# A hybrid diffusion backbone on one core: the heads of the differential form first, and the latent form's preparation beside them through one PSUM bank

## What is computed

```python
def mla_mixer(...):                     # latent form
    q = (rms_norm(c_q, g_q) @ w_uq).reshape(B, L, 4, 64 + 32)
    kv = (rms_norm(c_kv, g_kv) @ w_ukv).reshape(B, L, 4, 64 + 64)
    q_nope, q_rope = q[..., :64], q[..., 64:]
    k_nope, v = kv[..., :64], kv[..., 64:]
    # rope_2d on q_rope and k_rope for latent tokens; k_rope is shared by the heads
    # softmax(q k^T * 96 ** -0.5) v, per head
def diff_mixer(...):                    # differential form
    lam = exp(sum(lq1 * lk1)) - exp(sum(lq2 * lk2)) + lambda_init
    # 8 sub-heads of 32: rope_2d on q and k for latent tokens, softmax for each
    o = o[:, :, 0] - lam * o[:, :, 1]   # two sub-heads make one head
```

## Time and profile before

| what | value |
|---|---|
| median of 3 runs | 3166.14 us (3163.36 to 3167.25) |
| the profiled execution's own time | 3168.7 us |
| its span | 3166.9 us |
| PE, DVE, ACT, POOL busy | 80%, 62%, 37%, 36% of the span |
| attention block, layer 0 | 367.6 to 537.1 us |
| attention block, layer 1 | 2288.7 to 2395.0 us |

### The profile page before, as it was taken

How to read it: one execution, slowest core, us unless ns; L and a number is a source line. 1 busy time by engine, 2 the same in 40 slices (tenths; PEclk the granted TensorE clock), 3 DMA queues, 4 the chain that set the end, 5 groups by cost and what they waited for, 6 DMA issues and landing times. The chain is left out here.

```text
span 3166.9 us, 41622 instructions
## 1 busy us (share of the span) xinstructions
PE 2542.6 (80%) x15562; PEld 1901.4 (60%) x15562; DVE 1975.4 (62%) x4467; ACT 1168.2 (37%) x2244; POOL 1133.9 (36%) x1013
## 2 busy tenths in 40 slices
PE   5978699899166777888789999888777797777776
PEld 3778546587166777777678777577745552222222
DVE  3566535478896899877744444466543799845544
ACT  3422235327682333333333333342234443333332
POOL 1024100331006676566565555202303354433331
PEclk8985689899598898998899999888678899999999
DMA  5210141147039999999999999631002799999996
GB/s 206 77 31 1 62 160 36 60 150 251 0 166 381 407 406 403 365 384 397 390 400 406 405 406 405 242 97 31 9 1 90 302 415 422 421 422 422 421 421 247
DMA packets 211896, 816.93 MB, mean 258 GB/s; under 512 B 22680, under 2 KB 41688, under 8 KB 178032
## 3 DMA queue, kind: packets, MB, share of 16 engines
q0 software_dynamic: 110592, 536.92, 41.9%
q1 hardware_dynamic: 101104, 277.35, 23.5%
HBM read 796.37 MB, written 17.83 MB: 257 GB/s over the span
## 5 line engine op out<-in xcount | busy, mean ns | idle before, releaser
L1978 PE MATMUL ps<-pair_ring,pair_diag 128*128 128x512 f32 x1024 | 476.3, 610 | 144.4 <-ACT pair_diag L2052 141.7
L2162 DVE CUSTOM_DVE_ANT_0 pair_ring<-pair_ring,hT 128x1024 f32<-128x1024 f32 x256 | 313.1, 1223 | 212.0 <-DMA pair_ring<-in_uv_rows,eid 203.7
L1978 PEld LDWEIGHTS ps<-pair_ring,pair_diag 128*128 128x128 f32 x1024 | 187.2, 192 | 423.4 <-ACT pair_diag L2052 227.5
L1942 POOL DMA_INDIRECT pair_ring<-in_uv_rows,eid x256 | 267.4, 1045 | 391.7 <-PE ps L1978 366.8
L2310 POOL DMA_INDIRECT sparse_ring<-in_v_rows,eidT x256 | 286.0, 1117 | 294.9 <-PE ps L2359 223.0
L2310 POOL DMA_INDIRECT sparse_ring<-in_u_rows,eid x256 | 349.2, 1364 | 113.9 <-issue 67.5
L119 PE MATMUL ps<-h_hi,peer_uh 128*128 128x256 f32 x1024 | 310.6, 303 | 83.7 <-DVE peer_ul L2422 76.0
L2448 DVE CUSTOM_DVE_ANT_0 sparse_ring<-sparse_ring,hT 128x1024 f32<-128x1024 f32 x256 | 303.8, 1222 | 40.4 <-DMA sparse_ring<-in_u_rows,eid 32.9
L120 PE MATMUL ps<-h_lo,peer_uh 128*128 128x256 f32 x1024 | 300.0, 293 | 1.1 <-issue 1.1
L121 PE MATMUL ps<-h_hi,peer_ul 128*128 128x256 f32 x1024 | 299.3, 292 | 0.0
L119 PEld LDWEIGHTS ps<-h_hi,peer_uh 128*128 128x128 f32 x1024 | 206.8, 202 | 147.3 <-DVE peer_ul L2422 94.9
(11 more groups left out here) (413 smaller groups left out, 5437.6 us busy)
## 6 DMA issues: line engine op xcount, KB each, us to landing
peer_u<-in_uT SPq DMA_DIRECT2D x128, 512.0 KB
peer_v<-in_v_rows SPq DMA_DIRECT2D x128, 512.0 KB
ada_slab<-in_ada_w SPq DMA_DIRECT2D x20, 2048.0 KB, 9.1
proj_slab<-in_w_fm SPq DMA_DIRECT2D x38, 512.0 KB
route_slab<-in_w_pq SPq DMA_DIRECT2D x32, 512.0 KB, 6.9
peer_gates<-dense_stage SPq DMA_DIRECT2D x4, 4096.0 KB, 13.1
peer_gates<-peer_gates SPq DMA_DIRECT2D x32, 512.0 KB
out_slab<-in_w_out SPq DMA_DIRECT2D x16, 512.0 KB, 3.7
```

The lines of the kernel that those rows point to most:

```text
L1942: nc.gpsimd.indirect_dma_start(out=ring[:, s % R], out_offset=None, in_=d["uv_rows"], in_offset=bass.IndirectOffsetOnAxis(ap=eid[:, s:s + ...
L1978: mm = nc.tensor.matmul(ps[:, 4 + 2 * t + half, :], diag[:, s % DG, :], ring[:, s % R, D_MODEL + half * BANK:D_MODEL + (half + 1) * BANK], ...
L2162: nc.vector.tensor_tensor_reduce(out=row, in0=row, in1=hT[:, s // NS], scale=1.0, scalar=0.0, op0=ALU.mult, op1=ALU.add, accum_out=dots[:, ...
```

## The change

1. The differential form's units come first (n < `ND`), then the latent form's. The modulation columns in layer 0 move along with the latent form, to units 17 to 27.
2. Of the preparation only four rotations (through banks 4 and 5), squares, sums (banks 6 and 7) and roots stay in front of the first scores. SP loads the lambda parameters first.
3. The two reciprocals and the products with the norm's gain stand in DVE's list between the maxima and diagonals of units 0 to 2.
4. The fifth rotation, the 12 up-projections and the four query rotations are 17 items in a fixed order. A table `at` gives each its place (n, p) in the differential form's units: p = 0 is behind turn(n), 1 behind scores(n+2), 2 behind values(n-1). All go through bank 7: each waits on PE until the item before it has been read out of the bank. ACT and DVE have the evacuations at the same places in their lists. In layer 0 items 0 to 12 stand at (1, 0) to (13, 0), the four value projections in iterations 14 and 15. In layer 1 there are two or three in each of iterations 1 to 4, two in each of 5, 6 and 7.
5. All outputs use bank 6, by turns in partitions 0 to 63 and 64 to 127.

The core of the diff:

```diff
+            ND = HEADS * nt
+            ncomp = [2 if n < ND else 1 for n in range(NUN)]
...
+            items = [(ROT, 4)] + [(QK, n) for n in range(HEADS)]
+            for n in range(HEADS):
+                items += [(ROT, 5 + n), (QK, HEADS + n)]
+            items += [(QK, 2 * HEADS + n) for n in range(HEADS)]
+            slots = [(n, p) for n in range(1, ND - 2) for p in range(3)]
+            at = [slots[i * len(slots) // 13] for i in range(13)] + [(ND - 2 + i // 2, 1 + i % 2) for i in range(4)]
+            item_at = {x: items[i] for i, x in enumerate(at)}
+            before = {items[i]: items[i - 1] for i in range(1, len(items))}
...
-                ada_units = {1 + 3 * i // 2: i for i in range(ada.n)} if ada else {}
+                ada_units = {ND + 1 + 3 * i // 2: i for i in range(ada.n)} if ada else {}
...
                     def _(pe):
+                        turn_pairs(0, 4)
+                        turn_pairs(1, 5)
                         pe.wait_ge(sq_done, 1)
+                        nc.tensor.matmul(ps[:, 6, lo:], ones[:], sq[:, 0, lo:], start=True, stop=False)
...
+                        for n in (2, 3):
+                            pe.wait_ge(rot_ev, n - 1)
+                            turn_pairs(n, 4 + n % 2)
+                        pe.wait_ge(turned_in, 1)
+                        pe.wait_ge(root_done, 1)
+                        def item(x):
+                            if x not in item_at:
+                                return
+                            it = kind, n = item_at[x]
+                            if it in before:
+                                pe.wait_ge(*evacuated(before[it]))
...
-                        pe.wait_ge(prep_done, 1)
-                        pe.wait_ge(qk_ev, 3 * HEADS)
                         def scores(n):
-                            if ada and n == HEADS * nt:
-                                pe.wait_ge(ada_added, ada.part + 1)
+                            if n == ND:
+                                pe.wait_ge(prep_done, 1)
+                                pe.wait_ge(qk_ev, 2 * HEADS)
...
                         for n in range(NUN):
                             turn(n)
+                            item((n, 0))
                             if n + 2 < NUN:
                                 scores(n + 2)
+                            item((n, 1))
                             if n:
                                 values(n - 1)
+                            item((n, 2))
...
                         maxima(0)
                         maxima(1)
+                        lam_rest()
+                        root(0, lo)
                         diagonals(0)
+                        root(1, 0)
                         for n in range(NUN):
                             if n + 1 < NUN:
                                 diagonals(n + 1)
+                            item((n, 0))
                             if n + 2 < NUN:
                                 maxima(n + 2)
+                            if n == 0:
+                                normed()
+                            item((n, 1))
+                            item((n, 2))
```

More of the change, by code:

```diff
@@ L1190, in _, with turn_pairs @@
                     def _(pe):
-                        pe.wait_ge(sq_done, 1)
[L1192 to L1199, removed]
+                        def turn_pairs(n, bank):
+                            rows, x = rots[n]
+                            nc.tensor.matmul(ps[rows, bank, 0:SEQ], rotp[rows, rows], x, start=True, stop=True).then_inc(rot_mm, 1)
@@ L1281, in _ @@
+                        for n in range(4):
+                            last = turn_pairs(n, 4 + n % 2)
+                        last.then_inc(turned_in, 1)
+                        dve.wait_ge(lam_in, 16)
                         step(nc.vector.tensor_tensor(lamp[:], lamr[:, 0:4:2], lamr[:, 1:4:2], ALU.mult))
                         nc.vector.tensor_reduce(lame[:], lamp[:], AX, ALU.add).then_inc(lam_e, 1)
-                        dve.wait_ge(lam_x, 1)
-                        step(nc.vector.tensor_tensor(nlam[:], lame[:, 1:2], lame[:, 0:1], ALU.subtract))
@@ L1285, in _ @@
-                        step(nc.vector.tensor_scalar(nlam[:], nlam[:], -lam_init, None, ALU.add))
-                        dve.wait_ge(root_done, 2)
-                        nc.vector.reciprocal(rs[:, 0, lo:], rs[:, 0, lo:])
-                        step(nc.vector.reciprocal(rs[:, 1], rs[:, 1]))
-                        for x, g, r in ((fm[:, CQ0, lo:], gq[:, 0:1], rs[:, 0, lo:]), (fm[0:64, CQ1, lo:], gq[0:64, 1:2], rs[0:64, 0, lo:]),
-                                        (fm[:, CKV, :], gkv[:], rs[:, 1])):
-                            last = nc.vector.scalar_tensor_tensor(out=x, in0=x, scalar=g, in1=r, op0=ALU.mult, op1=ALU.mult)
@@ L1293, in _, with item @@
-                        last.then_inc(n_done, 1)
-                        for n, (rows, x) in enumerate(rots):
-                            dve.wait_ge(rot_mm, n + 1)
-                            nc.vector.tensor_tensor(rot[rows, n % 2], ps[rows, 4 + n % 2, 0:SEQ], sinT[rows], ALU.mult).then_inc(rot_ev, 1)
-                            step(nc.vector.tensor_tensor(x, x, cosT[rows], ALU.mult))
-                            dve.wait_ge(rot_ev, n + 1)
-                            last = nc.vector.tensor_tensor(x, x, rot[rows, n % 2], ALU.add)
+                        def item(x):
+                            kind, n = item_at.get(x, (None, 0))
+                            if kind != ROT:
+                                return
+                            last = turn_pairs(n, 7)
@@ L1339, in _ @@
                                 diagonals(n + 1)
+                            item((n, 0))
                             if n + 2 < NUN:
                                 maxima(n + 2)
+                            if n == 0:
+                                normed()
+                            item((n, 1))
+                            item((n, 2))
+                            if ada and n == ND - 1:
+                                dve.wait_ge(exp_done, c0[ND])
+                                ada.clear(dve)
         def add_gated(l, k, which, src, lo, hi=T):
```

107 lines of the change are left out of this document (69 added, 38 removed).

## The result

The changed kernel takes **3134.54 us** (median of 4 runs, 3126.92 to 3138.19) against 3166.49 us before (4 runs, 3163.36 to 3167.25): ratio 0.9898, 95% interval 0.9885 to 0.991. In a later measurement it took 3129.57 against 3166.2 us, ratio 0.9887 (0.9872 to 0.9902). The profiled execution's span is 3134.2 us.

What follows compares the result with a forecast made beforehand. PE bounds the units at full clock; in the preparation engines take turns, and idle PE drops to half clock. Savings of 19.4 us (layer 0) and 14.7 (layer 1), together 34.1, took 3166.1 to 3132 us, range 3122 to 3148.

Steps and rivals of the forecast that it cites:

- front to first scores: From each block's start to the first differential scores: 9.2 us in layer 0, 7.3 in layer 1.
- start-up to turn(3), turn(2): First scores to turn(3) in layer 0, 24 us, and to turn(2) in layer 1, 23 us, with DVE's list as bound.
- differential units, items, hand-overs: Remaining differential units with projections among them: 41.3 + 14.2 + 1.2 us in layer 0, 24.4 + 10.3 + 3.0 in layer 1.
- latent half and end: Latent units and block end: 59.3 + 0.9 us in layer 0, 21.1 + 2.5 in layer 1.
- The middle of two ends: Layer 0's front: 10.7 us with sums at low clock, 7.6 at full clock, so 9.2 was taken.
- the prediction's own list: Signs of being right or wrong; one wrong sign: PE waits for ACT at layer 1's up-projections over 3 us in all.
- Items: Projections and rotations among PE-bound differential units: 14.2 us in layer 0 that nothing hides, 10.3 in layer 1.
- Bank 6: ACT reading one partition half while PE writes the other: at most 10 us in all, taken as 0.
- Hand-overs through one bank: Rival: bank 7 waits cost 0.6 us at each of 27 other items, 16 us come back: 3148; chance 0.15.
- The clock stays down: Rival: start-up idling and bank 7 waits keep PE at 1.2 GHz in differential units, 3222 us at worst; chance 0.04.
- The swinging clock of the Trainium skill: Skill page cited under the low-clock rival: brief PE idling between PSUM bank groups swings the clock; the change would lose.
- The clock never falls: Rival: fronts at their short end, some 6 us less in start-up and hand-overs: 3124 us; chance 0.06.

## Why the prediction was right

The forecast was 3132 us, in a range of 3122 to 3148; measured 3134.54. The sum of the terms was 34.1 us for the two blocks, and 33.9 came out, by terms that lie within 1.5 us each. That the sum is right to 0.2 us is luck: layer 0 was put 1.9 us too long and layer 1 2.1 us too short.

| term | forecast, layer 0 | measured | forecast, layer 1 | measured |
|---|---|---|---|---|
| front to first scores | 9.2 | 7.8 | 7.3 | 6.6 |
| start-up to turn(3), turn(2) | 24 | 24.7 | 23 | 24.4 |
| differential units, items, hand-overs | 56.7 | 55.9 | 37.7 | 39.2 |
| latent half and end | 60.2 | 59.8 | 23.6 | 23.6 |
| block | 150.1 | 148.2 | 91.6 | 93.7 |

*Front.* The middle of two ends was the wrong choice: two rotations ahead keep the clock at 1.00, the sums take 1.12 us a pair, and the short end holds (written as 7.6 and 6.7, measured 7.8 and 6.6). Without them it is 13.0 and 10.7. The doubt stood in the step, and the experiment settles it.

*Start-up.* The list of DVE sets it, and the first turning came 7.6 us after the scores in layer 0, as written. For layer 1 the list was right too, and it gave the wait for the evacuation at the second query projection; what the step left out is that this wait (2.71 us) lowers the clock again. Start-up is 1.4 us over its term, and the turning behind the wait, 3.78 instead of 2.05 us, makes the 1.5 us in the next row. The copies moved later give back 4.6. By the prediction's own list this was a sign of being wrong: PE waits for ACT at the up-projections of layer 1 for 3.9 us in all (2.71, and 0.61 and 0.60 at the values), over its mark of 3.

*Items.* 14.2 us unhidden was right: PE is busy for 54.04 of 54.6 us, and doubling the key products costs 3.2 of the 3.4 us that they take. The hand-overs cost less than was charged. In layer 0 it is 0.56 and 0.12 us at the value projections, 0.7 against 1.2. In layer 1, from turning 2 on, it is 0.61, 0.64, 0.61 and 0.60, 2.5 against 3.0.

*Bank 6.* The latent head with three modulation blocks takes 502.47 - 485.06 = 17.41 us by its turnings, 17.4 in the earlier trace rows. Sharing the bank by partition halves costs nothing that can be seen, so 0 was right.

```profile
485.06 0.69 PE L1279 MATMUL ps<-diag,probs 128*128 128x128 f32 x4
...
502.47 0.69 PE L1279 MATMUL ps<-diag,probs 128*128 128x128 f32 x4
```

*The rivals.* Hand-overs through one bank: it did not come. Beside the waits of 0.92 and 2.71 us in layer 1 PE waits at bank 7 some 0.6 us four times there and once in layer 0, not at 27 more places. The clock stays down: it did in the start-up, for some 20 us of layer 0, and not beyond the third turning; in layer 1 the second fall lasts from about 2292.9 to 2299.5 us. (The rival's "within about 5 us" is not what the earlier trace rows shows, which is 8 us at 0.50 behind the preparation.) The swinging clock of the Trainium skill ("TensorE: Matmul & The Clock Gate", "A second HAM failure mode: psum-queue depth-cycling") does not show among the units, where PE goes through the banks at 1.00 for 54.6 us; layer 1's second fall comes behind one wait of 2.71 us, not behind many short ones. The clock never falls: it did fall, and even with spare products it is at 0.50 for some 3 us behind the front, and the block gains only 2.1. As an account of the cause, "PE waited and ran at half clock" holds: filling the waits of the preparation in the old kernel gives 14.6 of the 33.9 us, and 19.3 are left for moving the work. The two were not shown to add up, since the changed kernel has a low stretch of its own.

## What to carry to other kernels

When a stage alternates between engines, lay out each engine's list and see which of it the next stage does not need: what can run beside work that is full of PE costs only its own time there. A wait of PE costs more than its length when the clock falls in it, so price the work behind a wait at both levels, and look for some small useful work to put into it. DVE's order in the start-up deserves the most care: 1.4 us of copies moved behind one unit's maxima gave 4.6 in layer 1.

## What was not expected of the hardware

- **The query projections kept the high clock and did not bring it back.** Behind a wait of 0.81 us the projections with 96 and 64 columns of weights ran at 1.03 us a pair for 512 columns. Behind 4.13 us the eight query pairs ran at 2.02 us each without a break, from 387 to 401 us, and the clock came back at 403.4, among the key projections. It did so there in the kernel before, too (at 406.3), and with the items in front (at 403.1). The spare products with 128 columns, in the changed kernel's start-up, saw the clock fall at 374 and come back at 377. What decides between these cases was not tried and stays open.
- GpSimd's power of -1 is some 25 times as long as DVE's reciprocal, 82.15 against 3.35 us for 128x512.
- DVE's reciprocal in pieces costs 0.97 us for 128 columns, so 3.9 for 512, against 3.35 in one.
